# The experts' second product: the last 128 dense tokens with gates as weights, five partial sums of 512 in place of eight of 320

## The reference, cut to what matters

```python
# x: (b, T, 1024); 1024 prompt tokens and 8 x 16 sample tokens, 1152 in all
h2 = rmsnorm(x, norm2_g) * (1 + scale2) + shift2
x = x + gate2 * peer_ffn(h2, peer_wq, peer_keys, peer_u, peer_v)
y = rmsnorm(x, final_g)

def one(tb):                                   # in peer_ffn, for a block of tokens
    ...                                        # 8 heads pick 16 experts each: eidx, and shares w
    act = jax.nn.gelu(jnp.einsum("thkd,td->thk", u[eidx], tb))
    return jnp.einsum("thk,thkd->td", w * act, v[eidx])
```

## Time and profile before

| | us |
|---|---|
| median of 3 runs | 5066.22 |
| lowest and highest of these | 5063.36, 5066.4 |
| span of the profiled execution, first to last instruction | 5064.7 |
| TensorE busy in it | 4590.9 (91%) |
| VectorE busy in it | 3575.1 (71%) |
| ScalarE busy in it | 1803.4 (36%) |
| GpSimd busy in it | 1491.3 (29%) |

### The profile page before, as it was taken

One profiled execution on the slowest core, in us unless ns is written; L12 is line 12 of the kernel. 1 busy time (PEld: TensorE's weight loads), 2 busy tenths in 40 slices (PEclk: granted clock), 3 DMA queues, 4 the chain that ended last, 5 costly groups with the idle time before them and its releaser, 6 DMA issues. The chain is left out here.

```text
span 5064.7 us, 83501 instructions
## 1 busy us (share of the span) xinstructions
PE 4590.9 (91%) x28775; PEld 4257.5 (84%) x28775; DVE 3575.1 (71%) x6872; ACT 1803.4 (36%) x3737; POOL 1491.3 (29%) x1358
## 2 busy tenths in 40 slices
PE   7999999688887889997988577999999999999996
PEld 5999999677777559896877467999999999999995
DVE  3101555454554552344899997999999999999998
ACT  3111333232322553123444594333333333333332
POOL 0000000111110000000000003777777777777773
PEclk9999999888888779997989799999999999999998
DMA  4332222223332324433989457999999999999996
GB/s 158 120 134 91 83 88 93 112 91 110 108 107 75 71 60 154 178 140 126 340 326 333 180 195 287 373 361 376 373 369 380 378 372 376 378 374 371 375 373 255
DMA packets 350789, 1170.25 MB, mean 231 GB/s; under 512 B 40128, under 2 KB 91456, under 8 KB 344256
## 3 DMA queue, kind: packets, MB, share of 16 engines
q0 software_dynamic: 147456, 536.94, 28.2%
q1 hardware_dynamic: 160480, 483.07, 26.4%
q10 hardware_dynamic: 42720, 148.52, 7.7%
HBM read 971.20 MB, written 197.46 MB: 231 GB/s over the span
## 5 line engine op out<-in xcount | busy, mean ns | idle before, releaser
L2202 POOL DMA_INDIRECT ex_vr<-in_expert_v,ex_at x512 | 603.9, 1180 | 239.8 <-issue 153.4
L2200 POOL DMA_INDIRECT ex_ur<-scr_u_rows,ex_at x512 | 569.1, 1111 | 286.3 <-issue 118.1
L2389 DVE SCALAR_TENSOR_TENSOR ex_acc_rows<-ex_vr,ex_wt,ex_acc_rows 128x1024 f32<-128x1024 f32 x512 | 648.8, 1277 | 0.8 <-ACT ex_wt L2305 0.2
L2381 DVE SCALAR_TENSOR_TENSOR ex_ur<-ex_ur,h_rows 128x1024 f32<-128x1024 f32 x512 | 614.9, 1216 | 26.4 <-DMA ex_ur<-scr_u_rows,ex_at 25.5
L2194 POOL COPY ex_at<-picked_at 128x4 uint32 x128 | 106.4, 832 | 1495.1 <-POOLq L125 1494.6
L933 POOL TENSOR_TENSOR sd_cts<-sd_cT,sd_ea 128x512 f32<-128x512 f32 x72 | 92.5, 1285 | 1434.1 <-ACT sd_ea L891 1434.1
L2212 PE MATMUL ex_ps<-hd_hi,ex_u_hi 128*128 128x320 f32 x2048 | 469.7, 311 | 22.2 <-PEq L125 16.4
L2212 PE MATMUL ex_ps<-hd_lo,ex_u_hi 128*128 128x320 f32 x2048 | 469.6, 311 | 0.0
L2212 PE MATMUL ex_ps<-hd_hi,ex_u_lo 128*128 128x320 f32 x2048 | 468.7, 310 | 0.0
L2303 ACT ACTIVATE ex_gel<-ex_dot 128x1 f32<-128x1 f32 x512 | 103.6, 202 | 894.8 <-DVE ex_ur L2381 894.8
L479 DVE TENSOR_TENSOR pr_w_lo<-pr_w,pr_w_hi 128x1024 fp32r<-128x1024 f32 x56 | 68.6, 1225 | 489.6 <-ACT pr_w_hi L475 489.6
(11 more groups left out here) (357 smaller groups left out, 11370.1 us busy)
## 6 DMA issues: line engine op xcount, KB each, us to landing
pk_raw_u<-in_expert_u SPq DMA_DIRECT2D x128, 512.0 KB, 6.3
scr_u_rows<-pk_rows_u ACTq DMA_DIRECT2D x128, 512.0 KB, 6.1
ex_u<-in_expert_u SPq DMA_DIRECT2D x128, 512.0 KB, 6.7
ex_v<-in_expert_v SPq DMA_DIRECT2D x128, 512.0 KB, 8.3
scr_gate<-gt_stage SPq DMA_DIRECT2D x10, 4096.0 KB, 12.6
ex_gate<-scr_gate SPq DMA_DIRECT2D x32, 1280.0 KB, 8.9
pr_w<-in_w_main SPq DMA_DIRECT2D x58, 512.0 KB, 4.6
scr_xbc<-pr_out ACTq DMA_DIRECT2D x32, 576.0 KB, 3.8
```

Source lines behind the costliest of these rows:

```text
L2200: nc.gpsimd.indirect_dma_start(out=ur[:, s], out_offset=None, in_=scr["u_rows"], in_offset=by).then_inc(ur_in[s], 16)
L2202: nc.gpsimd.indirect_dma_start(out=vr[:, s], out_offset=None, in_=io["expert_v"].rearrange("j i d -> (j i) d"), in_offset=by).then_inc(vr_ ...
L2381: v.scalar_tensor_tensor(out=ur[:, s], in0=ur[:, s], scalar=1.0, in1=rows[:, s], op0=ALU.mult, op1=ALU.mult, accum_out=dot[:, m:m + 1]).th ...
L2389: v.scalar_tensor_tensor(out=acc_g[:, s], in0=vr[:, s], scalar=wt[:, m:m + 1], in1=acc_g[:, s], op0=ALU.mult, op1=ALU.add).then_inc(row_r[ ...
```

## The change

The dense tokens are cut into 512 (`WIDE`) and the last 128, instead of two halves of 320. For the 512, V stays the stationary operand: one matmul of 512 columns for each block of d, each e and each of the three split products (`wide_tokens`), into `kept` for the first four blocks and into `pv` for the other four. For the last 128 tokens the operands change places: the gates of these 128 tokens are the stationary operand, and V is the moving one, 512 values of d at a time (`late_tokens`). The result is [token, d] in place of [d, token]. The half with the lower d stays in PSUM over all batches (`kept_late`, now one bank of 512), the upper half is a fifth piece. So a batch has five pieces of 512 and five additions of 512, into `sums`, the same memory as `acc` in another shape. A batch's order on TensorE becomes: for each of four blocks the kept matmuls, a piece, and two steps of the U product; at the end the two halves of the late tokens. On VectorE five additions take places among the same other work.

In `finish_output` the dense part of x is 512 tokens wide, the late tokens come by one more transpose for each block of d (five in place of four), and VectorE reads 512 prompt tokens from the transposes' PSUM in place of 384.

```diff
-    LATE = TD - WIDE
-    SUMS = 2 * (KD - KEPT)
+    SUMS = KD - KEPT + 1
...
+        sums = acc[:].rearrange("p k t -> p (k t)").rearrange("p (j t) -> p j t", t=WIDE)
...
-            kept, kept_late = pb2("ex_kept", [P, KEPT, WIDE]), pb2("ex_kept_late", [P, KEPT, LATE])
+            kept, kept_late = pb2("ex_kept", [P, KEPT, WIDE]), pb2("ex_kept_late", [P, WIDE])
...
-                def keep(d, r, first, last):
+                def wide_tokens(out, d, r, first, last):
                     for e in range(E):
                         for x, y in SPLIT:
-                            w = v2[x][:, e, d * P:(d + 1) * P]
-                            nc.tensor.matmul(kept_late[:, d], w, g2[y][:, r, e, WIDE:TD], ...)
-                            nc.tensor.matmul(kept[:, d], w, g2[y][:, r, e, 0:WIDE], ...)
+                            mm = nc.tensor.matmul(out, v2[x][:, e, d * P:(d + 1) * P], g2[y][:, r, e, 0:WIDE], ...)
+                    return mm
+                def late_tokens(out, half, r, first, last):
+                    for e in range(E):
+                        for x, y in SPLIT:
+                            mm = nc.tensor.matmul(out, g2[y][:, r, e, WIDE:TD], v2[x][:, e, half * WIDE:(half + 1) * WIDE], ...)
+                    return mm
                 def piece(b, j, r):
-                    d, c = KEPT + j // 2, j % 2
                     pe.wait_ge(sum_r, b * SUMS + j + START)
-                    for e in range(E):
-                        for x, y in SPLIT:
-                            last = nc.tensor.matmul(pv[:, 0:HW], v2[x][:, e, d * P:(d + 1) * P], g2[y][:, r, e, c * HW:(c + 1) * HW], ...)
+                    if j < KD - KEPT:
+                        last = wide_tokens(pv[:], KEPT + j, r, True, True)
+                    else:
+                        last = late_tokens(pv[:], 1, r, True, True)
                     last.then_inc(sum_mm, 1)
...
-                    keep(0, r, first, last)
-                    piece(b, 0, r)
-                    u_products(0, 1)
-                    piece(b, 1, r)
...
+                    for d in range(KEPT):
+                        wide_tokens(kept[:, d], d, r, first, last)
+                        piece(b, d, r)
+                        u_products(2 * d, 2 * d + 1)
+                    late_tokens(kept_late[:], 0, r, first, last)
+                    piece(b, KEPT, r)
...
-                    a = (j % 2) * HW
-                    v.tensor_tensor(acc[:, j // 2, a:a + HW], acc[:, j // 2, a:a + HW], pv[:, 0:HW], ALU.add).then_inc(sum_r, 1)
+                    v.tensor_tensor(sums[:, j], sums[:, j], pv[:], ALU.add).then_inc(sum_r, 1)
...
                     add_rows(b, 2)
+                    add_rows(b, 3)
                     add_sums(b, 1)
-                    add_rows(b, 3)
                     if next_:
                         apply_gate(b + 1, 0, g + r, 1 - r)
-                    add_sums(b, 2)
                     dots(b, 4)
                     if more:
                         rest_of_u(b + 2, 0)
-                    add_sums(b, 3)
+                    add_sums(b, 2)
                     add_rows(b, 4)
                     dots(b, 5)
-                    add_sums(b, 4)
                     if next_:
                         rest_of_g(b + 1, 0, 1 - r)
                     add_rows(b, 5)
-                    add_sums(b, 5)
+                    add_sums(b, 3)
                     dots(b, 6)
                     dots(b, 7)
                     add_rows(b, 6)
-                    add_sums(b, 6)
                     if more:
                         rest_of_u(b + 2, 1)
                     add_rows(b, 7)
-                    add_sums(b, 7)
+                    add_sums(b, 4)
...
+                half, at = k // (KD // 2), k % (KD // 2) * P
+                nc.tensor.transpose(pst[:, k % 2, 0:P], late_sums[half][:, at:at + P], ident)
                 for s in range(ST):
-                    last = nc.tensor.transpose(pst[:, k % 2, s * P:(s + 1) * P], acc_g[:, s, k * P:(k + 1) * P], ident)
+                    last = nc.tensor.transpose(pst[:, k % 2, (s + 1) * P:(s + 2) * P], acc_g[:, s, k * P:(k + 1) * P], ident)
```

More of the change, by code:

```diff
@@ L2215, in u_product, with piece @@
                         last.then_inc(mm[e], 1)
-                def keep(d, r, first, last):
+                def wide_tokens(out, d, r, first, last):
                     for e in range(E):
                         for x, y in SPLIT:
-                            w = v2[x][:, e, d * P:(d + 1) * P]
[L2222 to L2226, removed]
-                    d, c = KEPT + j // 2, j % 2
-                    pe.wait_ge(sum_r, b * SUMS + j + START)
+                            mm = nc.tensor.matmul(out, v2[x][:, e, d * P:(d + 1) * P], g2[y][:, r, e, 0:WIDE],
+                                                  start=first and e == 0 and (x, y) == SPLIT[0], stop=last and e == E - 1 and (x, y) == SPLIT[-1], skip_group_check=True)
+                    return mm
+                def late_tokens(out, half, r, first, last):
                     for e in range(E):
                         for x, y in SPLIT:
-                            last = nc.tensor.matmul(pv[:, 0:HW], v2[x][:, e, d * P:(d + 1) * P], g2[y][:, r, e, c * HW:(c + 1) * HW],
-                                                    start=(e == 0 and (x, y) == SPLIT[0]), stop=(e == E - 1 and (x, y) == SPLIT[-1]))
+                            mm = nc.tensor.matmul(out, g2[y][:, r, e, WIDE:TD], v2[x][:, e, half * WIDE:(half + 1) * WIDE],
+                                                  start=first and e == 0 and (x, y) == SPLIT[0], stop=last and e == E - 1 and (x, y) == SPLIT[-1], skip_group_check=True)
+                    return mm
+                def piece(b, j, r):
+                    pe.wait_ge(sum_r, b * SUMS + j + START)
+                    if j < KD - KEPT:
+                        last = wide_tokens(pv[:], KEPT + j, r, True, True)
+                    else:
+                        last = late_tokens(pv[:], 1, r, True, True)
                     last.then_inc(sum_mm, 1)
@@ L2345, in _ @@
                     act.wait_ge(dot_r[s], BATCHES * 2 + START)
-                nc.scalar.copy(early[:, :, 0:WIDE], kept[:])
-                nc.scalar.copy(early[:, :, WIDE:TD], kept_late[:]).then_inc(early_r, 1)
+                nc.scalar.copy(early[:, 0:KEPT], kept[:])
+                nc.scalar.copy(early[:, KEPT], kept_late[:]).then_inc(early_r, 1)
             @block.vector
@@ L2451, in _, with finish_output @@
                 dve.wait_ge(early_r, 1 + START)
-        finish_output(nc, io, per, scr, [early[:, k] for k in range(KEPT)] + [acc[:, k] for k in range(KD - KEPT)], acc_g, x_first, x_in, fg)
-def finish_output(nc, io, per, scr, acc, acc_g, x_first, x_in, fg):
-    LP = SEQ - TD
+        finish_output(nc, io, per, scr, [early[:, k] for k in range(KEPT)] + [sums[:, k] for k in range(KD - KEPT)], (early[:, KEPT], sums[:, KD - KEPT]), acc_g, x_first, x_in, fg)
+def finish_output(nc, io, per, scr, acc, late_sums, acc_g, x_first, x_in, fg):
+    WIDE = TD - P
+    LP = SEQ - WIDE
     with ExitStack() as ctx:
@@ L2484, in _ @@
                 dve.wait_ge(x_in[k], 32 + START if k == 0 else 16 + START)
-                v.scalar_tensor_tensor(out=x[k][:, 0:TD], in0=acc[k], scalar=g, in1=x[k][:, 0:TD], op0=ALU.mult, op1=ALU.add)
+                v.scalar_tensor_tensor(out=x[k][:, 0:WIDE], in0=acc[k], scalar=g, in1=x[k][:, 0:WIDE], op0=ALU.mult, op1=ALU.add)
                 dve.wait_ge(turned, k + 1 + START)
@@ L2488, in _ @@
                     dve.wait_ge(x_r, k - 1 + START)
-                v.tensor_tensor(late[:, b].rearrange("p (b t) -> p b t", t=TS), pst[:, b, LP:].rearrange("p (b t) -> p b t", t=TS),
+                v.tensor_tensor(late[:, b].rearrange("p (b t) -> p b t", t=TS), pst[:, b, LP:LP + P].rearrange("p (b t) -> p b t", t=TS),
                                 per_token(mod[:, 5 * KD:6 * KD], k), ALU.mult).then_inc(scaled, 1)
-                v.scalar_tensor_tensor(out=x[k][:, TD:SEQ], in0=pst[:, b, 0:LP], scalar=g, in1=x[k][:, TD:SEQ], op0=ALU.mult, op1=ALU.add)
+                v.scalar_tensor_tensor(out=x[k][:, WIDE:SEQ], in0=pst[:, b, 0:LP], scalar=g, in1=x[k][:, WIDE:SEQ], op0=ALU.mult, op1=ALU.add)
                 dve.wait_ge(scaled, k + 1 + START)
```

17 lines of the change are left out of this document (3 added, 14 removed).

## The result

The changed kernel takes 5167.34 us (median of 4 runs, 5164.11 to 5174.08) beside 5066.31 for the kernel before on the same chip: ratio 1.0195, 95% interval 1.0176 to 1.0213. It is 101 us slower; the forecast was 13 faster. Its profiled execution took 5169.66 us with a span of 5167.5.

A forecast was written before the change was run, and what follows sets the result against it. VectorE was taken as the bound, TensorE 0.1 us a batch behind. Steady batches -11.6, batch 62 -1.7, batch 63 -2.3, tail +1.2 gave -14.4; 1 us returned to late gathers made -13, 5053 us; range 5046 to 5065.

The forecast's parts named there:

- working of TensorE and VectorE: Experts' stage, each batch: TensorE falls 1.4 us to 27.9, worth nothing; VectorE falls 0.19 us to 29.25.
- rival 2: TensorE, experts' stage: a 512-column matmul costs 0.28 us, not 0.23; +87 us, 5153; chance 7%.
- the two idle places: TensorE, each batch: idle some 1.3 us in all, ahead of the first sum and after the first piece.
- Rival 3: TensorE, experts' stage: its clock drops to half for a tenth of each batch; +62 us, 5128; chance 4%.
- Rival 4: Experts' stage: TensorE is the bound today, so its whole 87 us would be won; 4979; chance 3%.
- rival 5: At VectorE's additions: a TensorE lead is too small, VectorE waits about 0.2 us a batch; no change, 5065; 6%.
- The failed step: Gathers on GpSimd: distances between freeing and rereading buffers unchanged, except one 0.2 us shorter; no DMA added or moved past another.
- the sign: VectorE's waits for gathered U rows: growth by about 10 us would show the prediction wrong.
- Rival 1: Experts' stage: gathers give the pace, VectorE's 0.19 us only becomes waits for U rows; -2.8 us, 5063; chance 13%.
- The ends: Stage's first and last batches: batch 0 nothing, batch 62 -1.7 us, batch 63 -2.3 us; tail +1.2 us.
- The tail: After the experts' stage: eight more transposes and wider reads at either end cost +1.2 us.

The follow-up runs named there:

- e1: Changed kernel with the small copies of the rows' shares moved from GpSimd to ScalarE; 5094.99 us, ratio 1.0057 to the kernel before.
- e7: Changed kernel with both the shares' copies on ScalarE and VectorE's split of U in two halves; 5052.43 us, ratio 0.9963.
- e3: Kernel before, with two more small copies for each half batch on GpSimd into an unused buffer; 5178.95 us, ratio 1.0215.
- e2: Changed kernel with VectorE's split of U made in two halves of 512 columns; 5078.37 us, ratio 1.0024 to the kernel before.
- e4: Changed kernel with the fifth sum added before the last split of U, not at the batch's end; 5147.62 us, ratio 1.0160.
- e9: Changed kernel with each addition of 512 cut into two of 256, strewn over VectorE's list; 5152.51 us, ratio 1.0177.
- e8: Changed kernel with VectorE's splits of U and of V both made in halves; 5138.92 us, ratio 1.0141 to the kernel before.

## Why the prediction was wrong

Its working of TensorE and VectorE held. TensorE after the change:

```profile
3611.48 0.47 PE L2222 MATMUL ex_kept<-ex_g_hi,ex_v_hi 128*128 128x512 f32 x1 [0.67 <-DVE ex_g_lo L2363]
...
3612.91 0.39 PE L2222 MATMUL ex_pv<-ex_g_hi,ex_v_hi 128*128 128x512 f32 x1
3613.14 0.39 PE L2222 MATMUL ex_pv<-ex_g_lo,ex_v_hi 128*128 128x512 f32 x1
...
3614.92 0.53 PE L2213 MATMUL ex_ps<-hd_hi,ex_u_hi 128*128 128x320 f32 x2 [0.48 <-ACT ex_act L2284]
```

The 512s stand at 0.23, so rival 2 fell; the two idle places are the ones named, ahead of the first sum and behind the first piece. Rival 3 fell too: the granted clock is 0.97 in the stretch and TensorE waits for VectorE's additions (70.6 us), not the reverse (5.7). VectorE's addition takes 0.60 to the next start (3606.91 to 3607.51), and clean batches of e1 take 29.22 to 29.23, where 29.25 was forecast. Rival 4 and rival 5 fell with them.

**The failed step** is the one on the gathers: "between the dots that free a buffer and those that read it again the distances are unchanged" and "No DMA is added or moved past another on SP or POOL". It looked at when a gather may start and never at how long GpSimd needs for one, and that depends on what VectorE runs beside it. Rearranging VectorE's list rearranged those meetings: 2.3 us a batch more for the same gathers (149.5 us over 64 batches), nearly all of the 2.4 by which GpSimd's need grew, from some 28.3 to 30.7. It had some 1.6 to spare. With its need past VectorE's 29.25, GpSimd gave the pace; it still waited about 1.1 us a batch for VectorE (53.4 and 5.7 us in 54 batches), so the batch of 31.49 is longer than either engine's own work. The prediction named the sign itself: waits for U rows that grow by about 10 us. They grew by 96.

Rival 1 named the right engine's work and dismissed it by the right row read the wrong way: 84 us of waiting on GpSimd was taken to show that buffers hold the gathers back, when it was also the margin: 1.6 us a batch for U rows and 1.0 for V rows, the gaps included. Its price was bounded at "VectorE's 0.19 only turns into waits"; no loss was priced. Two sums of the prediction don't come out either, and neither bears on the miss: with its bounds of 0.15 and 0.20 and 0 to 4 us of gathers its range starts at 5051, not 5047, and its chances add up to 0.63 faster, 0.26 same and 0.11 slower.

The ends were nearly right. Batch 62 and 63 on VectorE, and the copies on ScalarE (as the earlier trace rows), then the chain that ended last (as the earlier trace rows):

```profile
5059.40 1.21 DVE L2367 TENSOR_TENSOR ex_v_lo<-ex_v,ex_v_hi 128x1024 fp32r<-128x1024 f32 x1
...
5071.35 1.23 DVE L2377 SCALAR_TENSOR_TENSOR ex_ur<-ex_ur,h_rows 128x1024 f32<-128x1024 f32 x1 [1.70 <-DMA ex_ur<-scr_u_rows,ex_at]
...
5088.35 1.21 DVE L2367 TENSOR_TENSOR ex_v_lo<-ex_v,ex_v_hi 128x1024 fp32r<-128x1024 f32 x1
...
5114.64 0.68 DVE L2371 TENSOR_TENSOR ex_acc<-ex_acc,ex_pv 128x512 f32<-128x512 f32 x1
```

```profile
5114.54 0.59 ACT L2344 COPY h_rows<-ex_kept_late 128x512 f32<-128x512 f32 x1
```

```profile
5116.14 0.45 PE fo_pst L2511
5116.59 0.87 PE fo_pst L2513 x4
```

Batch 62 took 28.95; without its wait of 1.70 for a gather 27.25 (forecast 27.4). The last addition now ends after the copies, as forecast. From the last batch's first split to the next phase's first transpose it is 27.79 us, before 29.77: -2.0 (forecast -2.3). The tail from there to the end is 51.4, before 49.1: +2.3, where 1.2 was forecast. The spans differ by 102.8: +105.3 in the 63 periods, -2.8 ahead of them, +0.3 behind.

With room made on GpSimd the gain is there: e7's median batch is 29.37, before 29.54, with 0.13 us a batch more on VectorE. That e7's 5052.43 lies beside the 5053 of the forecast is in part luck, as e7 has these other edits and its mean batch, 29.66, still holds late gathers.

Shown are GpSimd as the bound (e1, e3, e7), the hold-ups one by one (timelines) and that shortening the largest group returns most of the loss (e2). Not settled are which place of an addition does the most harm, and where e4's 20 us come from. The two lists of VectorE differ in nothing but the additions, eight of 0.40 at eight places and five of 0.60 at five; e4 and e9, which change these places, moved the hold-ups more than they removed them.

## What to carry to other kernels

Before you reorder an engine's list, ask which engine runs beside it and whether its instructions have a length of their own: here the neighbour's instruction set that of the gathers, and the places of a few additions made 150 us of it. An engine's waits for the bound are its margin; write them down by batch (here at most 2.57 of 29.8 us, and some 1.6 without the gaps that stand there anyway) and price what uses them up, even for an engine that the change doesn't touch. Where two engines block each other by whole instructions, shorter ones on the bound can pay (0.13 us a batch bought 89 us in e2), but measure it: the same cut made elsewhere as well (e8) cost some 60.

## What the hardware showed that was not expected

A gather instruction takes 0.94 us when it begins in an addition from PSUM (326 cases in the two kernels, held up by 0.011 us at most) and up to 1.98 behind one SBUF instruction of 1.14. Some gathers of about 5 us miss the ends of up to five VectorE instructions that follow each other without a gap (31 in e8, 19 in e9, none after). The Trainium skill (SBUF — State Buffer, SBUF: two separate sides) gives the port pair to the one that starts first. Taken for a gather that is waiting already, that would have given it to the gather of e8 at 3522.58, and the measurement says otherwise. In the tail, one more transpose in each group and wider reads cost 2.3 us, and not the 1.2 that the added instructions were estimated at; what makes the other 1.1 wasn't tried.
